# One launch of a hybrid decoder block: the prologue's loads and tiles in another order, and the conv's banks read out ahead of its sigmoid

## The reference

```python
h = rmsnorm(x, mix_norm_g)
u = h @ w_in                                  # mq mk mv mo mi mf gq gk gv gr ga
qk = silu(causal_conv(concat([mq, mk]), conv_w, conv_b))     # 4 taps over rows
h_m = mlstm_chunkwise(mq, mk, mv, log_i, log_f)              # state C, n, m
h_g = gla_chunkwise(gq, gk, gv, log_a)                       # state S
x = x + concat([head_norm(h_m) * sigmoid(mo), head_norm(h_g) * silu(gr)]) @ w_out
mn = rmsnorm(mem, mem_norm_g); K = mn @ wk_x; V = mn @ wv_x
x = x + softmax((rmsnorm(x) @ wq_x) K^T / 16) V @ wo_x       # 4 heads of 256
x = x + square(relu(rmsnorm(x) @ w1)) @ w2
out = rmsnorm(x)
```

## Time and profile before

| what | value |
|---|---|
| median of 3 runs | 3004.27 us (3002.13 to 3004.37) |
| the profiled execution's own time | 3005.62 us |
| its span, first to last instruction | 3004.1 us |
| TensorE busy | 2948.6 us |
| VectorE, ScalarE, GpSimd busy | 1577.8, 1256.1, 358.8 us |
| mean granted clock of TensorE | 0.994 of full |

### The profile page before, as it was taken

One profiled execution on the slowest core, in us unless ns is written; L12 is line 12 of the kernel. 1 busy time (PEld: TensorE's weight loads), 2 busy tenths in 40 slices (PEclk: granted clock), 3 DMA queues, 4 the chain that ended last, 5 costly groups with the idle time before them and its releaser, 6 DMA issues.

```text
span 3004.1 us, 44428 instructions
## 1 busy us (share of the span) xinstructions
PE 2948.6 (98%) x15836; PEld 2438.1 (81%) x15836; DVE 1577.8 (53%) x2805; ACT 1256.1 (42%) x2470; POOL 358.8 (12%) x619
## 2 busy tenths in 40 slices
PE   6999999999999999999999999999999999999998
PEld 6878788888887888888887878888888788888886
DVE  5375645444566655443457564544456665544444
ACT  5554444333445344432435444433344533443233
POOL 2253100000023300000005310000002430000000
PEclk9999999999999999999999999999999999999999
DMA  5732132433242122323234212243324212232332
GB/s 170 254 99 70 57 92 85 134 98 98 91 156 78 58 78 92 127 92 105 91 95 151 71 55 89 90 134 98 94 96 151 82 57 78 90 99 92 98 98 77
DMA packets 151604, 301.73 MB, mean 100 GB/s; under 512 B 13808, under 2 KB 13936, under 8 KB 151408
## 3 DMA queue, kind: packets, MB, share of 16 engines
q1 hardware_dynamic: 139776, 262.38, 28.3%
q0 software_dynamic: 8960, 31.47, 2.8%
q10 hardware_dynamic: 2672, 5.28, 0.5%
HBM read 282.27 MB, written 16.81 MB: 100 GB/s over the span
## 4 chain that ended last, share of the span: by engine, by line
PE 91%; DVE 4%; ACT 2%; issue 2%; DMA 1%; SPq 0%; DVEq 0%; ACTq 0%; POOL 0%
PE bank L1530 54%; PE work L1530 27%; PE work L1544 2%; DVE qk L1293 1%; PE work L1634 1%; PE bank L1581 1%; PE work L1672 1%; PE bank L1544 1%; PE work L1686 1%; PE work L1697 1%; PE work L1714 1%; PE work L1779 1%; PE work L1797 0%; PE work L1796 0%; SPq L428 0%
## 5 line engine op out<-in xcount | busy, mean ns | idle before, releaser
L1059 DVE TENSOR_TENSOR w_lo<-raw,w_hi 128x512 fp32r<-128x512 f32 x912 | 633.2, 699 | 1265.7 <-ACT w_hi L630 1265.1
L630 ACT ACTIVATE w_hi<-raw 128x512 fp32r<-128x512 f32 x976 | 610.1, 631 | 1437.0 <-PE bank L1530 903.3
L1530 PE MATMUL bank<-act_hi,w_hi 128*128 128x512 f32 x992 | 392.6, 396 | 0.3
L1530 PE MATMUL bank<-act_lo,w_hi 128*128 128x512 f32 x992 | 386.7, 390 | 0.0
L1530 PE MATMUL bank<-act_hi,w_lo 128*128 128x512 f32 x992 | 386.4, 390 | 0.0
L1530 PE MATMUL bank<-w_hi,h_hi 128*128 128x512 f32 x736 | 290.7, 395 | 0.0
L1530 PE MATMUL bank<-w_hi,h_lo 128*128 128x512 f32 x736 | 286.9, 390 | 0.0
L1530 PE MATMUL bank<-w_lo,h_hi 128*128 128x512 f32 x736 | 286.8, 390 | 0.0
L1530 PE MATMUL bank<-w_hi,act_hi 128*128 128x512 f32 x640 | 264.7, 414 | 13.7 <-ACT gqkv L934 13.7
L1530 PE MATMUL bank<-w_hi,act_lo 128*128 128x512 f32 x640 | 253.1, 396 | 0.0
L1530 PE MATMUL bank<-w_lo,act_hi 128*128 128x512 f32 x640 | 252.5, 395 | 0.0
(11 more groups left out here) (307 smaller groups left out, 4873.0 us busy)
## 6 DMA issues: line engine op xcount, KB each, us to landing
raw<-in_w_dram SPq DMA_DIRECT2D x256, 512.0 KB, 3.7
raw<-in_w_in_dram SPq DMA_DIRECT2D x112, 512.0 KB, 3.6
raw<-in_w_out_dram SPq DMA_DIRECT2D x32, 512.0 KB, 3.8
raw<-kq_dram SPq DMA_DIRECT2D x32, 512.0 KB, 3.7
raw<-vo_dram SPq DMA_DIRECT2D x32, 512.0 KB, 3.7
xres<-in_x_dram POOLq DMA_DIRECT2D x16, 512.0 KB, 6.3
tok<-in_x_dram POOLq DMA_DIRECT2D x12, 512.0 KB, 8.2
out_dram<-xres POOLq DMA_DIRECT2D x12, 512.0 KB, 3.9
```

Of the source, the lines that this page charges most:

```text
L630: nc.scalar.activation(w_hi[:, slot, :], raw[:, pair_slot, slot % 2, :], ACT.Copy).then_inc(slab_hi, 1)
L1059: ins = tt(w_lo[:, slot, :], src, hi, ALU.subtract)
L1530: ins = mm(dst, left, right, start=(kt == 0 and j == 0), stop=(kt == KT - 1 and j == 2))
```

## The change

Prologue:
- The memory rows and `mem_norm_g` are loaded first in SP's queue instead of ScalarE's, into `mem_rows`, which is the space of `folded`, not of `xres`.
- GpSimd loads the x rows before it builds the masks, without a wait; the 28 small transfers leave SP and are issued by GpSimd behind the masks. ScalarE waits for them at slab 18 (`X_SLAB`); the gate weights are copied at slab 27 (before: 13).
- ScalarE splits one slab instead of three ahead of `guess`, VectorE one behind the row scales. Four memory tiles are turned ahead of slab 0, the others one each in slabs 0 to 3.
- Squares of x rows: slabs 4 to 7, one each (before: four at slab 10). Scaling: slabs 10 to 13, one each (before: four at slab 10). x tiles: slabs 18 to 25 (before: 16 to 23).
- The first two turns of `wq_x` stand at slabs 29 and 30, later ones two ahead of their fold (before: one ahead, the first behind slab 31). `fold_kq` writes `wbank[2]` and `wbank[3]` by turns, so it waits for the read-out two folds back (before: four banks, four back) and no longer for `kv_lo` of the last block.

In every group:
- ScalarE reads MQ's and MK's banks ahead of the sigmoid of that slab, copies `halo` in front of the four tiles in one instruction and the tails back in another. VectorE's two halo copies per tile and its wait for the read-out are gone.
- The last update of `stC` stands ahead of the split of slab 40.
- `MIX_SLABS`: tiles 4, 5, 6, 7 at slabs 58, 59, 60, 61 (before: 4 and 5 at 58, 6 and 7 at 59).

```diff
-MIX_SLABS = {53: (0,), 54: (1, 2), 55: (3,), 58: (4, 5), 59: (6, 7)}
+MIX_SLABS = {53: (0,), 54: (1, 2), 55: (3,), 58: (4,), 59: (5,), 60: (6,), 61: (7,)}
+X_SLAB = 2 * KT + 2
+        mem_rows = folded[:].rearrange("p (i r) n -> p i (r n)", r=2)
...
 # SP
+            for dst, src in ((mem_rows[:, 0, :], A["mem"][0:P, :]), (mem_rows[:, 1, :], A["mem"][P:2 * P, :]),
+                             (norm_g[:, 3, :], A["mem_norm_g"])):
+                sp.dma_start(dst, src).then_inc(mem_in, 16)
...
-                    if q == 2 * PAIRS:
-                        sp.wait_ge(zeroed, 1)
-                        for dst, src in small:
-                            sp.dma_start(dst, src).then_inc(const_in, 16)
...
 # GpSimd: x rows behind sel's two transfers, then the masks, then
-            pool.wait_ge(tok_ready, MEM // P)
-            for i in range(NCH):
-                pool.dma_start(xres[:, i, :], A["x"][i * P:(i + 1) * P, :]).then_inc(x_in, 16)
+            for dst, src in small:
+                pool.dma_start(dst, src).then_inc(const_in, 16)
...
 # ScalarE, prologue
             act.wait_ge(mem_in, 16 * 3)
             for i in range(2):
-                sum_squares(i)
-            for n in range(LEAD):
-                split_pro(n)
-            guess(2, 1)
-            for kt in range(KT):
+                sum_squares(i, mem_rows)
+            split_pro(0)
+            guess(2, 1)
+            for n in range(1, LEAD):
+                split_pro(n)
+            for kt in range(4):
                 tile_hi(kt, kt, MEM, 3, h_hi)
...
+                    if b == 0 and s < 4:
+                        tile_hi(4 + s, 4 + s, MEM, 3, h_hi)
                     if KT * b + s + LEAD < PRO_KV:
                         split_pro(KT * b + s + LEAD)
+                    if b == 0 and s >= 4:
+                        if s == 4:
+                            act.wait_ge(x_in, 16 * NCH)
+                        sum_squares(s - 4)
+                    if b == 1 and s == 1:
+                        guess(NCH, 2)
+                    if KT * b + s == X_SLAB:
+                        act.wait_ge(const_in, 16 * N_CONST)
+                    if 0 <= KT * b + s - X_SLAB < KT:
+                        kt = KT * b + s - X_SLAB
+                        tile_hi(KT + kt, kt, GROUP, 0)
+                    if b == 3 and s >= 6:
+                        turned_hi(s - 6)
...
 # TensorE, prologue
+            tiles_out(0, {0: [(tok_ready, 2)]}, 2, range(4))
             for b in range(4):
                 for kt in range(KT):
                     if b == 0:
                         pe.wait_ge(act_lo_ready, kt + 1)
+                        if kt < 4:
+                            tiles_out(0, {}, 2, [kt + 4])
+                    if 0 <= KT * b + kt - X_SLAB < KT:
+                        tiles_out(KT, {0: [(tok_ready, PRO_ROWS)]}, NCH, [KT * b + kt - X_SLAB])
+                    if b == 3 and kt == 5:
+                        pe.wait_ge(act_lo_ready, 2 * KT)
+                    if b == 3 and kt in (5, 6):
+                        turn_wq(kt - 5)
...
-                            ins = mm(bank[j % 4][:, hh * MEM:(hh + 1) * MEM], left, right,
+                            ins = mm(wbank[2 + j % 2][:, hh * MEM:(hh + 1) * MEM], left, right,
...
             for j in range(2 * KT):
-                if j + 1 < 2 * KT:
-                    turn_wq(j + 1)
-                pe.wait_ge(bank_free, U_KQ + j - 3 if j >= 4 else U_KQ)
+                if j + 2 < 2 * KT:
+                    turn_wq(j + 2)
+                if j >= 2:
+                    pe.wait_ge(bank_free, U_KQ + j - 1)
                 fold_kq(j)
...
 # ScalarE, group
+                    if b in (B_MQ, B_MK) and r == KT - 1:
+                        tails = halo[:, 4 * b:4 * b + 4, :]
+                        nc.scalar.activation(ubuf[b][:, :, 0:CONV - 1], tails, ACT.Copy).then_inc(halo_in, 1)
+                        for i in range(4):
+                            full(4 * b + i)
+                            nc.scalar.activation(ubuf[b][:, i, CONV - 1:], bank[i][:], ACT.Copy).then_inc(bank_free, 1)
+                        read_out(act, g, 4 * b + 3)
+                        act.wait_ge(halo_in, 4 * g + 2 * b + 1)
+                        nc.scalar.activation(tails, ubuf[b][:, :, GROUP:], ACT.Copy).then_inc(halo_in, 1)
...
 # VectorE, group
+                    if s == G_SLAB - 1:
+                        carry(NCH - 1)
                     split(g, s, scalar=s // KT in (1, 2))
...
-                            read_out(dve, g, k)
-                            mark(nc.vector.tensor_copy(ubuf[b - 1][:, i, 0:CONV - 1], halo[:, k, :]))
                             acc = qk[:, k, :]
-                            settle()
+                            if i == 0:
+                                dve.wait_ge(halo_in, 4 * g + 2 * b)
                             dve.wait_ge(conv_first, KT * g + k + 1)
...
-                            nc.vector.tensor_copy(halo[:, k, :], ubuf[b - 1][:, i, GROUP:]).then_inc(conv_done, 1)
+                            ins.then_inc(conv_done, 1)
```

More of the change, by code:

```diff
@@ L504, in _ @@
                 pool.dma_start(sel_raw[row:row + NGATE], sel_raw[0:NGATE]).then_inc(sel_spread, 16)
+            for i in range(NCH):
+                pool.dma_start(xres[:, i, :], A["x"][i * P:(i + 1) * P, :]).then_inc(x_in, 16)
             tmp = qk[:, 0, 0:P]
@@ L727, in _ @@
             for j in range(2 * KT + 1):
[L728 to L732, removed]
+                if 2 <= j < 2 * KT:
+                    turned_hi(j)
                 if j >= 1:
-                    fold_out(j - 1, U_KQ + j - 1, XHD ** -0.5)
+                    fold_out(j - 1, U_KQ + j - 1, XHD ** -0.5, wbank[2 + (j - 1) % 2])
                 if j > 2 * KT - LEAD:
@@ L1108, in _ @@
                        ALU.subtract).then_inc(gate_w_lo, 1)
-                if s == KT + 2:
+                if s == KT + 1:
                     row_scales(NCH, PRO_ROWS, 2)
[L1112 to L1115, removed]
+                if KT + 2 <= s < KT + 2 + NCH:
+                    scale_row(s - KT - 2, tok, xres)
+                if X_SLAB <= s < X_SLAB + KT:
+                    tile_lo(KT + s - X_SLAB, s - X_SLAB, GROUP, 0)
+                if s >= PRO_KV - 2:
+                    turned_lo(s - PRO_KV + 2)
                 if s % KT == KT - 1:
@@ L1123, in _ @@
             for j in range(2 * KT + 1):
[L1124 to L1127, removed]
+                if 2 <= j < 2 * KT:
+                    turned_lo(j)
                 if j > 2 * KT - LEAD:
@@ L1229, in group, with carry @@
                 nc.vector.memset(vext[:, :, :, HD:HD + 1], 1.0).then_inc(v_ones, 1)
+                def carry(c):
+                    dve.wait_ge(c_full, 4 * g + c + 1)
+                    upd = work[:, 0:2, :].rearrange("p b (h n) -> p (b h) n", h=2)
+                    if c >= 1:
+                        dve.wait_ge(c_ready, 4 * g + c)
+                    for h in range(HEADS):
+                        ins = stt(out=stC[:, h, :], in0=stC[:, h, :],
+                                  scalar=bc[:, 0, c * HEADS + h:c * HEADS + h + 1],
+                                  in1=upd[:, h, 0:HD + 1], op0=ALU.mult, op1=ALU.add)
+                    ins.then_inc(c_ready, 1)
                 for s in range(1, B_OUT * KT):
+                    if s == G_SLAB - 1:
+                        carry(NCH - 1)
                     split(g, s, scalar=s // KT in (1, 2))
@@ L1345, in group @@
                             nc.vector.tensor_copy(hden[:, c, :], num[:, :, HD]).then_inc(num_out, 1)
-                        if stage == 3:
-                            dve.wait_ge(c_full, 4 * g + c + 1)
-                            upd = work[:, 0:2, :].rearrange("p b (h n) -> p (b h) n", h=2)
-                            if c >= 1:
-                                dve.wait_ge(c_ready, 4 * g + c)
-                            for h in range(HEADS):
-                                ins = stt(out=stC[:, h, :], in0=stC[:, h, :],
-                                          scalar=bc[:, 0, c * HEADS + h:c * HEADS + h + 1],
-                                          in1=upd[:, h, 0:HD + 1], op0=ALU.mult, op1=ALU.add)
-                            ins.then_inc(c_ready, 1)
+                        if stage == 3 and c < NCH - 1:
+                            carry(c)
                     c, slot = divmod(s - G_SLAB, 3)
@@ L1568, in turn_wq @@
                 ins.then_inc(qt_full, 1)
+            tiles_out(0, {0: [(tok_ready, 2)]}, 2, range(4))
+            for b in range(4):
+                for kt in range(KT):
+                    if b == 0:
+                        pe.wait_ge(act_lo_ready, kt + 1)
+                        if kt < 4:
[6 more added lines that the diff above has]
+                        turn_wq(kt - 5)
+                    slab(KT * b + kt, kt, "feature", None if b == 0 else 4 * (b - 1), h_hi, h_lo, MEM)
             def fold_kq(j):
```

92 lines of the change are left out of this document (41 added, 51 removed).

## The result

The changed kernel takes 2966.1 us (median of 4 runs, 2964.2 to 2966.7) against 3004.0 us of the kernel before on the same chip: ratio 0.9872, 95% interval 0.9861 to 0.9884, so 34.8 to 41.8 us faster. The forecast was 2964.0, its range 2956 to 2982. The profiled execution has a span of 2964.1 us against 3004.1: 40.0 less by that pair, 37.9 by medians. The profiled execution of the kernel before (3005.6) lies 1.6 above that kernel's median, so where the two differ the medians count.

The account below looks back on a forecast made before the run. TensorE, busy 2948.6 of 3004.1 us, bounds the kernel, so gains come only from its idle or lower-clock time: 17.3 - 0.4 - 1.7 + 22.0 + 1.5 + 1.3 = 40.0; 3004.3 - 40.0 = 2964 us, range 2956 to 2982.

Parts of the forecast that it names:

- Conv, 22.0: MK to MV boundary, four groups: reading banks ahead of the sigmoid removes 13.7 us of waits and 8.3 of lower clock.
- 0.4 to 0.5 us of slack: Next boundary, MV: claimed to have this much slack, as in the kernel before.
- Rival B: The conv wait comes back at the MV boundary; if half of the 22 returns, 2975 us; chance 0.12.
- The clock, 8.3: After the conv waits: TensorE's clock below full in four windows, 8.6 us less 0.3 on idle time, claimed regained.
- Carry and mix, 2.8: Groups: TensorE's waits on `stC` (1.5 us) and on `gate_heads` at mix tile 5 (1.3) go.
- Start of the prologue: Before slab 0: gain lands at 7.0, first transpose at 12.5, first slab at 14.2 us instead of 20.8.
- Rival C: Prologue: memory rows land no sooner, the 4 KB gain being slow; 2.5 us less gained, 2967 us; chance 0.08.
- The slabs: Prologue's 32 slabs: block 1 from 27.1, block 2 from 39.1, `fold_kq(0)` at 67.7 instead of 85.06, 17.3 us gained.
- The constants, 1.7: 28 small transfers on GpSimd land at 47 against a limit of 45.3, delaying slab 24: loss 1.7 us, bounds 0 and 8.
- the unseen price: Issue cost of the two `w_in` transfers of 1,024 runs each, shown by no row: between 0.55 and 4.4 us.
- rival A: Prologue: constants land late by the 4.4 us price; loss 7 instead of 1.7 plus half clock, 2972 us; chance 0.17.
- The fold, 0.4: Prologue's `fold_kq`: waits of 0.1 per two folds, 0.7 in all, less 0.3 already paid: 0.4 us lost, upper bound 3.

Follow-up runs that it names:

- the filler: The kernel before plus 14 unused matmuls per group at slab 16, run while TensorE would wait for MK's banks; 2999.0 us, ratio 0.9983.
- e8_const_sp: The changed kernel with the 28 small transfers issued by SP at their old place, ahead of the first wv pair; 2974.3 us.
- e10_fold_first: The changed kernel with each later turn of `wq_x` (j+2) behind fold j instead of ahead of it; 2963.7 us, ratio 0.9868.
- e2_prologue: The kernel before with only the prologue part of the change, the groups left old; 2992.8 us, ratio 0.9965.
- e12: The changed kernel with turns of `wq_x` behind their folds and the squares of x rows spread over slabs 5, 7, 9, 11; 2964.5 us, ratio 0.9871.
- e9: The changed kernel measured again, unchanged, on the chip of the last experiments; 2966.8 us, ratio 0.9876.

## Why the prediction was right, and where its reasons were not

**The size.** The total was 40.0 against 37.9 measured. Inside, two terms are off against each other: the groups were forecast at 24.8 and gave 26.3, the prologue at 15.2 and gave 11.6. That the total is so near is in part luck, since the two misses have opposite signs. That the spans of the two profiled executions differ by exactly 40.0 is luck altogether, since the one before is a late execution.

**Conv, 22.0.** The size was right: groups alone 26.3, less 3.2 for carry and mix, is 23.1. The step of the prediction that was to give it was not. "Now the read-out stands ahead of that wait ... the 3.4 is gone" makes the order the cause, and VectorE's copies a by-product; the order alone returns 1.7 (not clear of nothing), the copies alone 17.3, the two together 23.1. The number came out because the change held both. VectorE enters the conv late, and with steps of 5.40 against 5.45 it stays so; without the copies the step is 4.80 (0.6 off, where I had put 0.85), and what it has not caught up by MK's end (1.0 us a group) the order carries across that boundary, to be worked off in MV. The "0.4 to 0.5 us of slack" at MV was that of a schedule already delayed by the wait. Rival B's mechanism was thus real, and the lighter VectorE, its "against" sentence, is what kept it away.

**The clock, 8.3.** Right in the main: the filler returns 4.3 net of a new wait of 3.0, so 7.3, and all windows are full in the kernel after.

**Carry and mix, 2.8.** Right as far as the interval goes: 3.2, 0.3 to 6.0.

**Start of the prologue.** The gain landed at 6.5 (forecast 7.0), the first transpose came at 12.66 (12.5). Rival C, the late gain, is thus wrong. `guess` stands behind a split whose pair landed only at 9.4, which is the 0.16 by which the first transpose is late. The rest of slab 0's delay, 15.15 for 14.2, is the transposes ahead of it: ten in 2.49 us, where I had 1.7 for a tile and a split. Slab 0 itself then took 1.95 instead of 1.44 (below).

**The slabs.** Block 1 at 29.32 for 27.1. I had left out that the squares of x rows, moved into block 0, load ScalarE beside its splits; the first boundary's wait is 1.5 us instead of 0.5 (spreading them takes 0.3 of it away). `fold_kq(0)` came at 69.87 for 67.7, 2.2 late.

**The constants, 1.7.** Landed at 47.0 as forecast, cost nothing: the slabs that they would have held were 2.6 us late themselves. The 28 issues ran from 27.09 to 43.58 (forecast 25.8 to 41.2, or 48.9 by the upper price); two sorts of row in GpSimd's timeline bear on the unseen price:

```profile
28.73 0.54 POOL L529 DMA_DIRECT2D conv_b<-in_conv_b_dram  x1
...
30.34 1.79 POOL L529 DMA_DIRECT2D qk<-in_w_in_dram  x2
```

The ones with 1,024 runs took 0.90 us each, against 0.54 for a plain one: the low end of 0.55 to 4.4 was nearly right, and rival A with it wrong. The Trainium skill ("DMA: Bandwidth & Descriptors", the section on the anatomy of a GpSimd DMA) has many descriptors emitted before the cost shows; 1.7 times the time for eight times the runs agrees in the main. Its "Issuing engine by pattern" calls SP's queue generally faster; the issues agree (12.3 us for the 28 on SP in `e8_const_sp`, 16.5 on GpSimd), but this did not decide here: that kernel is 8.2 us slower, because of what stood behind the transfers in the queue.

**The fold, 0.4.** This is, for its size, the term most mis-sized: 1.9 (31.7 for 29.8). The prediction had named a fold's step well over 1.92 as a sign of being wrong, and it is 2.03. I had the wait nearly right, 0.12 where I put 0.1 per two folds, but took a wait to cost its length. Each also costs 0.19 in the transposes behind it, which `e10_fold_first` takes back whole.

So the prologue: by the profiles of the old one (82.6 to 85.1, mean 83.5) and of the new one (69.9, 70.7, 69.5, mean 70.0) `fold_kq(0)` gained 13.5, where 17.3 less 1.7 for the constants, 15.6, was forecast. Of the 2.1 that are missing 1.5 are the late execution (85.06 for 83.5) and 0.6 the slabs. The folds then lost 1.9 instead of 0.4. The VO stage, from the last fold to the first gate matmul, is the same within the spread of the profiles (22.8 to 23.7 us in the six old ones, 22.4 to 23.9 in the three new ones). That is 11.6 for 15.2.

## What to carry to other kernels

When a wait shows one late releaser, compare that engine's step with the waiting engine's and look where its debt began before moving anything: if the steps are equal, as here, an earlier place in the program hands the debt to the next boundary, and it was less work on the late engine that paid it. Price a wait with what follows it: here 13.7 us of waiting brought 7 to 8 us of lower clock, and a wait of 0.12 us brought 0.19 us more. Before a part of a gain is read off a pair of profiles, compare the same stretch in other profiles of unchanged code: here the old prologue alone varied by 2.3 us between executions. With work turned two steps ahead into few buffers, issue the step that consumes first and the one that refills behind it.

## What the runs showed of the hardware that was not expected

- The first matmuls of slab 0 stand nearly twice as far apart as later ones, though the clock column reads full (1.00 from 12 to 18). In TensorE's timeline of the kernel after, matmuls of 256 columns in slab 0 stand 0.21 us apart, and from the seventh on 0.12:

```profile
15.38 0.41 PE L1560 MATMUL bank<-h_hi,w_lo 128*128 128x256 f32 x1
15.59 0.41 PE L1560 MATMUL bank<-h_hi,w_hi 128*128 128x256 f32 x1
...
16.34 0.28 PE L1560 MATMUL bank<-h_lo,w_hi 128*128 128x256 f32 x1
16.46 0.28 PE L1560 MATMUL bank<-h_hi,w_lo 128*128 128x256 f32 x1
```

The spacing of 0.21 is also that of the kernel before where its granted clock reads 0.50 (56 to 57 us). In the kernel before, 16 transposes (3.7 us) instead of ten (2.5 us) stand ahead of slab 0, and its matmuls are 0.12 apart from the third on. Slab 0 took 1.95 us here, 1.77 in `e2_prologue` and 2.26 to 2.56 in e8 to e12 with the same start, instead of 1.44: up to 1.1 us that no wait shows, and most of why e9 is later than the kernel after.

- VectorE and GpSimd may slow each other. In the kernel before, VectorE's splits from `raw` at 179.64 and 180.84 took 0.67 us each while one GpSimd instruction, whose like take 0.39 to 0.93, lasted 2.34 (from 179.45); at 185.93 a split took 0.90 and GpSimd's instructions beside it 0.84 to 0.86. But the split at 184.52 took 0.68 with GpSimd at its usual pace (0.92). The Trainium skill ("SBUF — State Buffer", "SBUF: two separate sides") has the two share a port and lock each other out; the durations agree with it in part, and no run here changed GpSimd's work alone, so the cause is not shown.
